# A hybrid decoder layer in fp32: the first activations in eight pieces, and an up projection with stationary weights

## The reference

```python
h = rms_norm(x, ln_mix_w)                      # x: 256 x 2048
proj = h @ w_in                                # 2048 x 9216, the first product
...                                            # pooling branch, HGRN2 branch, gates, w_out
h2 = rms_norm(x, ln_ffn_w)
u = causal_depthwise_conv(h2 @ w_up, conv_w, conv_b)   # 2048 x 11008, 3 taps over tokens
u_gate, u_val = jnp.split(u, 2, axis=-1)
x = x + (jax.nn.silu(u_gate) * u_val) @ w_down         # 5504 x 2048
h3 = rms_norm(x, ln_ple_w)
x = x + jax.nn.sigmoid(h3 @ w_ple_gate) * (p @ w_ple)
return rms_norm(x, ln_final_w)
```

## Time and profile before

| | us |
|---|---|
| median of 3 runs (1482.78 to 1483.22) | 1483.19 |
| the profiled execution, its own time | 1483.09 |
| its span, first to last instruction | 1481.3 |
| PE busy in it | 1460.6 (99%) |
| DVE, ACT, POOL busy | 872.9, 744.3, 126.0 |

### The profile page before, as it was taken

One profiled execution on the slowest core, in us unless ns is written; L12 is line 12 of the kernel. 1 busy time (PEld: TensorE's weight loads), 2 busy tenths in 40 slices (PEclk: granted clock), 3 DMA queues, 4 the chain that ended last, 5 costly groups with the idle time before them and its releaser, 6 DMA issues.

```text
span 1481.3 us, 18755 instructions
## 1 busy us (share of the span) xinstructions
PE 1460.6 (99%) x6814; PEld 1218.5 (82%) x6814; DVE 872.9 (59%) x976; ACT 744.3 (50%) x913; POOL 126.0 (9%) x81
## 2 busy tenths in 40 slices
PE   7999999999999999999999999999999999999997
PEld 5888888888888888888888888888888888888886
DVE  4576676545454545556676666766767555454655
ACT  5555555444444444445555555555555444443544
POOL 1034143100000000000110110100101000000000
PEclk9999999999999999999999999999999999999999
DMA  7755555456666655556656556656555655555653
GB/s 235 248 150 153 159 155 148 144 165 186 197 186 194 189 195 184 190 178 192 184 177 193 184 177 196 181 181 196 175 181 176 202 194 190 196 188 184 223 196 121
DMA packets 189754, 271.88 MB, mean 184 GB/s; under 512 B 11380, under 2 KB 103112, under 8 KB 189568
## 3 DMA queue, kind: packets, MB, share of 16 engines
q1 hardware_dynamic: 189408, 270.88, 58.8%
q0 software_dynamic: 288, 0.21, 0.1%
HBM read 268.95 MB, written 2.10 MB: 183 GB/s over the span
## 4 chain that ended last, share of the span: by engine, by line
PE 97%; DVE 1%; ACT 1%; issue 1%; DMA 0%; POOL 0%; SPq 0%; ACTq 0%; POOLq 0%; DVEq 0%
PE main L528 30%; PE main L529 30%; PE main L530 30%; PE aux L553 3%; PE aux L600 2%; PE aux L634 0%; DMA x_tok<-in_x 0%; PE aux L624 0%; DVE cv L1145 0%; DVE w_lo L1002 0%; ACT w_hi L774 0%; DVE bT L1102 0%; POOL dec L1339 0%; ACT cv L882 0%; PE aux L614 0%
## 5 line engine op out<-in xcount | busy, mean ns | idle before, releaser
L1002 DVE TENSOR_TENSOR w_lo<-raw,w_hi 128x1024 fp32r<-128x1024 f32 x508 | 651.8, 1287 | 550.8 <-ACT w_hi L774 549.5
L774 ACT ACTIVATE w_hi<-raw 128x1024 fp32r<-128x1024 f32 x508 | 535.8, 1055 | 647.6 <-PE main L530 631.5
L528 PE MATMUL main<-w_hi,xT_hi 128*128 128x512 f32 (+1 forms) x1408 | 551.5, 392 | 4.3 <-DVE w_lo L1002 4.3
L530 PE MATMUL main<-w_hi,xT_lo 128*128 128x512 f32 (+1 forms) x1408 | 545.6, 387 | 0.0
L529 PE MATMUL main<-w_lo,xT_hi 128*128 128x512 f32 (+1 forms) x1408 | 545.6, 387 | 0.0
L528 PEld LDWEIGHTS main<-w_hi,xT_hi 128*128 128x128 f32 x1408 | 265.1, 188 | 58.0 <-issue 4.4
L530 PEld LDWEIGHTS main<-w_hi,xT_lo 128*128 128x128 f32 x1408 | 264.9, 188 | 54.4
L529 PEld LDWEIGHTS main<-w_lo,xT_hi 128*128 128x128 f32 x1408 | 265.2, 188 | 51.8
L528 PE MATMUL main<-w_hi,aT_hi 128*128 128x512 f32 x344 | 134.4, 391 | 0.1
L530 PE MATMUL main<-w_hi,aT_lo 128*128 128x512 f32 x344 | 133.9, 389 | 0.0
L529 PE MATMUL main<-w_lo,aT_hi 128*128 128x512 f32 x344 | 133.9, 389 | 0.0
(11 more groups left out here) (166 smaller groups left out, 913.5 us busy)
## 6 DMA issues: line engine op xcount, KB each, us to landing
raw<-in_w_up SPq DMA_DIRECT2D x336, 256.0 KB
raw<-in_w_in SPq DMA_DIRECT2D x144, 512.0 KB
raw<-in_w_down SPq DMA_DIRECT2D x84, 512.0 KB
raw<-in_w_out SPq DMA_DIRECT2D x32, 512.0 KB
raw<-in_w_ple_gate SPq DMA_DIRECT2D x32, 512.0 KB
raw<-in_w_branch_a SPq DMA_DIRECT2D x16, 512.0 KB
raw<-in_w_branch_b SPq DMA_DIRECT2D x16, 512.0 KB
x_tok<-in_x SPq DMA_DIRECT2D x4, 512.0 KB, 8.6
```

Of the source, the lines that this page charges most:

```text
L528: pe.matmul(acc, th, wh, start=first, stop=False)
L530: return pe.matmul(acc, tl, wh, start=False, stop=end)
L774: ac.activation(w_hi[:, u % RING, :, 0:w], raw[:, u % RING, :, 0:w], ACT.Copy).then_inc(hi_full, 1)
L1002: dve.tensor_tensor(w_lo[:, u % RING, :, 0:w], raw[:, u % RING, :, 0:w], w_hi[:, u % RING, :, 0:w].bitcast(F32), ALU.subtract).then_inc(lo ...
```

## The change

**Start.** x comes in eight pieces of 256 columns. SP issues piece 0 first of all, then unit 0 as two loads, then pieces and units in turn; the identity and the norm vector go through ACT's queue. PE does ten matmuls on a constant tile, `junk` (5, 3 and 2, around the first transposes), which nothing reads. The first unit is taken apart (`first_unit`): its first row tile runs product by product as its parts arrive. Piece i+2 is transposed in the middle of unit i.

**Up projection.** `xT_hi` and `xT_lo` become halves of one tile `xT`. In `up_rows` the weights are stationary, 128 columns at a time. `w_hi` meets hi and lo tokens side by side in one matmul of 512 columns, `w_lo` meets the hi tokens in one of 256. A unit is 8 matmuls of 512 and 8 of 256 columns. Results have features on partitions already, four banks for a chunk (all of `main` or all of `aux`, in turn), with the sum still in two halves: ACT copies one half out (`z`), DVE adds the other and multiplies by the row scale, which now varies along the free axis and is held in `rB` (made by two transposes on PE and one copy). The `z_tok` transposes are gone. The half-wide chunk is the first of the 22, not the last.

```diff
-    [(-2, "vec"), (-1, "xT0"), (0, "xT1"), (2, "xT2"), (4, "xT3"), (6, "cvec")]
+    [(-3, "vec"), (-2, "xT0"), (-1, "xT1")] + [(i - 2.5, f"xT{i}") for i in range(2, UK)] + [(6, "cvec")]
...
+    + [(UP + 5, "rB")]
     + [(P_T, "pT")]
...
+
+            def x_piece(i):
+                at = slice(i * FW, (i + 1) * FW)
+                sp.dma_start(x_tok[:, :, at], x_v[:, :, at]).then_inc(x_in[i], 16)
+
+            x_piece(0)
+            at = slice(PROJ[0], PROJ[0] + NCOL)
+            sp.dma_start(raw[:, 0, 0, :], w_in_v[:, 0, at]).then_inc(first_raw, 16)
+            sp.dma_start(raw[:, 0, 1, :], w_in_v[:, 1, at]).then_inc(raw_full[0], 32)
+            for u in range(1, 4):
+                x_piece(u)
                 rows(u, w_in_v, 2 * u, PROJ[0])
-                if u < NQ - 1:
-                    sp.dma_start(x_tok[:, :, cols(u + 1)], x_v[:, :, cols(u + 1)]).then_inc(x_in[u + 1], 16)
+            for i in range(4, UK):
+                x_piece(i)
             for u in range(4, MIX):
...
+            def first_row_tile():
+
+                wh, wl = w_hi[:, 0, 0, :], w_lo[:, 0, 0, :]
+                th, tl = ([t[:, 0, tb * P:(tb + 1) * P] for tb in range(TB)] for t in (xT_hi, xT_lo))
+                pe.wait_ge(xT_hi_ready, 1)
+                pe.wait_ge(first_hi, 1)
+                for tb in range(TB):
+                    pe.matmul(main_acc(0, tb), th[tb], wh, start=True, stop=False)
+                pe.wait_ge(first_lo, 1)
+                for tb in range(TB):
+                    pe.matmul(main_acc(0, tb), th[tb], wl, start=False, stop=False)
+                pe.wait_ge(xT_ready, 1)
+                for tb in range(TB):
+                    pe.matmul(main_acc(0, tb), tl[tb], wh, start=False, stop=False)
+
...
+            def up_rows(j, u, i, it=None, blocks=4):
+
+                pe.wait_ge(lo_full, plus(u + 1, 2 * UK, it))
+                if i == 0 and j:
+                    pe.wait_ge(z_read, plus(j, 2, it))
+                if i == 0 and j == 0:
+                    pe.wait_ge(x_new, 2 * (NQ - 1))
+                for a in range(2):
+                    k = 2 * i + a
+                    for b in range(blocks):
+                        pe.matmul(up_acc(j, b), w_hi[:, u % RING, a, b * P:(b + 1) * P],
+                                  xT[:, k, :, :].rearrange("p h t -> p (h t)"), start=(k == 0), stop=False)
+                    for b in range(blocks):
+                        mm = pe.matmul(up_acc(j, b)[:, 0:SEQ], w_lo[:, u % RING, a, b * P:(b + 1) * P], xT[:, k, 0, :],
+                                       start=False, stop=(k == KD - 1))
+                mm.then_inc(units_done, 1)
+
+            def rstd_rows():
+
+                pe.wait_ge(rstd_ready, 2)
+                for tb in range(TB):
+                    mm = pe.transpose(aux_flat("rB")[:, tb * P:(tb + 1) * P], rstd[:, 1, tb:tb + 1].to_broadcast([P, P]), ident[:])
+                mm.then_inc(aux_ready, 1)
+
...
+            def warm_up(n):
+
+                for _ in range(n):
+                    pe.matmul(main[:, 0, 0, 0:P], junk[:, 0:P], junk[:, 0:P], start=True, stop=True)
+
+            pe.wait_ge(junk_set, 1)
+            warm_up(5)
+            side("vec")
+            warm_up(3)
+            side("xT0")
+            warm_up(2)
+            side("xT1")
             u = 0
+            first_unit()
+            u = 1
             for c in range(C_MIX):
-                for i in range(UK):
...
                 if i == 0:
                     chunk_done(ac, C_UP + j, it)
-                    for tb in range(TB):
-                        ac.activation(z_tok[:, tb, 0:2 * nf * P], main_acc(C_UP + j, tb, 2 * nf * P), ACT.Copy,
-                                      scale=rstd[:, 1, tb:tb + 1]).then_inc(z_ready, 1)
-                if i == 2:
-
-                    name = f"zT{j:02d}"
-                    aux_arrived(ac, name, it)
+                    ac.activation(z[:, 0:2 * nf, :], up_acc(j, slice(0, 2 * nf))[:, :, SEQ:NCOL], ACT.Copy).then_inc(z_half, 1)
+                if i == 1:
+
+                    ac.wait_ge(z_ready, plus(j + 1, 2, it))
...
             def up_post(j, i, it=None):
-                nf = 2 if j < NUP - 1 else 1
+                nf = 2 if j else 1
                 f0 = lambda f: slice(f, f + 1) if it is None else bass.ds(it * 4 + f, 1)
+                if i == 0:
+
+                    dve.wait_ge(z_half, plus(j + 1, 2, it))
+                    zs, acc = z[:, 0:2 * nf, :], up_acc(j, slice(0, 2 * nf))
+                    dve.tensor_tensor(zs, acc[:, :, 0:SEQ], zs, ALU.add).then_inc(z_read, 1)
+                    dve.wait_ge(z_read, plus(j + 2, 2, it))
+                    dve.tensor_tensor(zs, zs, rB[:].rearrange("p (b t) -> p b t", b=1).to_broadcast([P, 2 * nf, SEQ]),
+                                      ALU.mult).then_inc(z_ready, 1)
                 if i == 2:
...
+                if s == UP + 3:
+                    inverse_rms(1)
+                if s == UP + 6:
+                    aux_arrived(dve, "rB")
+                    dve.tensor_copy(rB[:], aux_flat("rB")[:, 0:SEQ]).then_inc(z_read, 1)
...
```

More of the change, by code:

```diff
@@ L151 @@
     + [(out_slot(n) + 1, f"x1T{n}") for n in range(NQ)]
-    + [(up_slot(j) + 1, f"zT{j:02d}") for j in range(NUP)]
+    + [(UP + 5, "rB")]
     + [(P_T, "pT")]
@@ L280, in build @@
         aux_ready = sem("aux_ready")
[L282 removed]
+        x_in = [sem(f"x_in{i}") for i in range(UK)]
+        junk_set, first_raw, first_hi, first_lo = map(sem, ("junk_set", "first_raw", "first_hi", "first_lo"))
         const_in, vec_in, late_in, p_in, lnf_in, out_done = map(
@@ L781, in store, with hi_blocks @@
                     ac.activation(dst(tb), main_acc(c, tb), func, scale=rstd[:, norm, tb:tb + 1]).then_inc(done, 1)
-            def hi_blocks(name, dst, first, vec, done):
+            def hi_blocks(name, dst, first, vec, done, n=4):
                 aux_arrived(ac, name)
-                for b in range(4):
-                    ac.activation(dst[:, first + b, :], aux_blocks(name)[:, b, :], ACT.Copy,
+                src = aux_banks(name) if n == 2 else aux_blocks(name)
+                for b in range(n):
+                    ac.activation(dst[:, first + b, :], src[:, b, :], ACT.Copy,
                                   scale=vecT[:, vec + b:vec + b + 1]).then_inc(done, 1)
@@ L955, in _ @@
                         up_post(j - 1, i, it)
-            for s in range(DOWN - UK, UNITS - SPLIT_TB):
+            for s in range(DOWN, UNITS - SPLIT_TB):
                 slot(s)
```

183 lines of the change are left out of this document (109 added, 74 removed).

## The result

The changed kernel takes 1472.9 us (1471.42 to 1474.0), against 1483.2 before: a ratio of 0.9931, 95% interval [0.9917, 0.9944]. Repeated in a later session it took 1472.54 (1470.88 to 1474.12), 0.9930 [0.9917, 0.9944]. So it is 10.3 us faster. 16.3 were forecast, and the time lies 1.4 us above the range given.

The account below looks back on a forecast made before the run. PE's queue was taken to bound the kernel: 1483.1 - 11.2 (up projection) + 0.5 (waits with the half-wide chunk first) - 5.5 (start) = 1466.9 us, range 1462 to 1471.5.

Parts of the forecast that it names:

- Price of a matmul: Up projection on PE: 226.9 ns per 512-column and 119.8 ns per 256-column matmul, giving 22.19 us per full chunk.
- The paragraph on the operand layout: Up projection: stationary weights might expose weight loads, 188 instead of 120 ns per 256-column matmul; cost taken as 0.
- The observable I named: Up projection: 256-column matmuls at 150 ns or more would show the forecast wrong.
- Transposes gone: Up projection on PE: dropping the z_tok transposes saves 18.7 us.
- old stalls: Old half-wide chunk: PE's waits there disappear, saving 1.1 us.
- rB: Up projection on PE: two transposes for rB and the wait around them add 0.3 us.
- half-wide chunk: Now first in the up projection: 12.3 us of PE work, plus 0.5 us for new waits.
- Rivals 3 to 7: PE stalls 1469.4 (0.07); pieces useless 1472.4 (0.06); DVE bound 1511 (0.03); weight loads show 1561 (0.02); fixed cost vanishes 1431 (0.02).
- The start: Kernel start: first real matmul at about 8.3 us, first chunk ending at 35.3 instead of 40.8, a gain of 5.5 us.
- rival 1: Start gives only 3 us: first unit stays at 427 ns, x1 lands 1 to 1.5 us late; 1469.4 us, chance 0.13.
- rivals 1 and 4: Start: gives little, 1469.4 us, chance 0.13; or eight pieces of x bring nothing, 1472.4 us, chance 0.06.
- the term of 1.2 us: Start: PE's slow-clock stretch in the first unit, taken at half of the earlier 2.3 us.

Follow-up runs that it names:

- all_512: Changed kernel with every w_lo product taken over 512 columns instead of 256, so all matmuls of a unit have one size; 1612.68 us (one execution).
- all_256: Changed kernel with every 512-column matmul of the up projection cut into two of 256 with the same weights; 1485.69 us (one execution).
- no_junk: Changed kernel without the matmuls on the constant tile at the start; 1472.95 us.
- after_again: The changed kernel itself, unaltered, run once more on another chip; 1472.54 us.
- x_pair: Changed kernel with the second piece of x issued directly behind the first, ahead of the first rows of input weights; 1471.63 us.
- eight_a: Changed kernel with all eight 512-column matmuls of a unit first, then the eight of 256, rows as outer loop; 1470.1 us.
- still_x: Changed kernel with pieces of xT as stationary operand of the up projection in place of the weights, its result left out; 1472.26 us (one execution).
- moving_w: Changed kernel with w_hi as moving operand of the up projection in place of xT, its result left out; 1470.62 us (one execution).
- only_hi: Changed kernel without the 256-column matmuls, so the product with w_lo is left out of the up projection; 1419.02 us.

## Why the prediction was wrong, step by step

- **Price of a matmul: the step that failed.** "So a matmul costs its columns and some 13 ns on top" holds for streams of one size without a break, where I had read it (226.7 and 120.0 ns in `all_512` and `all_256`). The changed unit mixes the two, and I multiplied 64 x 0.2269 + 64 x 0.1198 without a bound for that. What the runs showed in its place is 232.4 and 118.5 ns, 33 ns more for a unit. The trace of before had the hint: 314, 232 and 231 ns behind the transposes, and 113 and 119 for the first two 256-column matmuls at 1122.18. I averaged over 45 matmuls that stand clear of both. The chunk is 22.46 and not 22.19: 5.6 us of the miss. The paragraph on the operand layout bounded the wrong thing, the weight load, and took 0, rightly for loads. The observable I named ("256-column matmuls at 150 ns or more") did not catch it; the other, 22.2 us a chunk, did.
- **Transposes gone, old stalls, rB, half-wide chunk**: right. The half-wide chunk took 12.66 us where the terms gave 12.3 + 0.5; the profile has no wait of PE there for rB or weights, and the two pauses of 0.2 us are most of the difference to 12.3. Rivals 3 to 7 did not happen. DVE took 16.3 us of a chunk, less than the 18.1 allowed.
- **The start: right in the middle execution, short in the profiled one.** The first chunk was forecast to end at 35.3; it ended at 35.12 in the middle of eleven executions, within 0.2, and at 36.70 in the one profiled for the changed kernel. That the gain is still 5.1 and 3.6 at the up projection, and not 5.7 and 4.1, is the new wait for `tok`: I looked for waits only up to the first chunk, and put what came behind it at nothing without a row. The landing of piece 1 at 7.3 was at the early end of what came (7.5 in `no_junk`, 9.22 in the changed kernel). I gave one number from one execution's curve, where a spread of 1.7 us belonged to it, and the range had only 1 to 1.5 us for it, in rival 1. Medians give 3.6 to 4.8, by which kernel they are taken against. The times of rivals 1 and 4 (1469.4, 1472.4) come nearer to the result than mine. Rival 1 did happen in part in the profiled execution (piece 1 landed 1.9 us late, the first row tile stayed at 427 ns), but most of the miss is in the loop, which neither of them touches.
- **Clock**: the term of 1.2 us was right in the profiled execution (slow spacing to 12.4) and near 0 in `after_again`. Neither mattered much, since a faster first row tile waits for piece 2. The Trainium skill (TensorE: Matmul & The Clock Gate, section What's actually happening) says that the moment of release varies from run to run; by that, the traces agree: the changed kernel's first four matmuls of that row tile took 1.86 us in one execution (10.08 to 11.94) and 1.01 in the other (8.69 to 9.70).
- **The 2.5 ns of the Trainium skill** (the same page, section Back-to-back issue gap, which gives it for isolated matmuls): one size alone gives 226.7 and 120.0 ns, 13 ns above the columns at 2.4 GHz, also with stationary weights. 2.5 ns is seen in no run here.
- **The range**: 1462 to 1471.5 took in waits and landings, but nothing for a matmul's price in the new mixture. The missing term has one sign in the changed kernel's order and in every other order tried (+13 to +53 ns a unit), and it takes the time out.

## What to carry to other kernels

A price read in a stream of equal instructions is a price for that stream. Look in the trace for what follows a break in it, too. Where a change mixes sizes, leave a term for it: here 33 ns a unit of 2.8 us, 1.2%, and try the orders that the program allows; eight and eight gave 2.8 us here, two and two in one accumulator 3.8. At a start, move first what PE waits for, then look at the next thing that lands: of three edits here none moved the end by more than the executions of one kernel differ among themselves. And before you credit an edit with a microsecond, see where in the trace it lies: in `x_pair` it lay in a loop that the edit hadn't touched.

## What the runs showed of the hardware that I had not expected

- The first five 512-column matmuls behind 256-column ones take 228 to 236 ns instead of 227 (`eight_a`), at a granted clock of 1.00 in the loop. With weights or x held, and x or w_hi streamed, the first four lie at 224 to 236 (`still_x`, `moving_w`). Behind a wait of PE it is much the same (224 to 240 in a unit of `only_hi`). A 256-column one just behind a 512 takes 113 to 119 instead of 120.
- One size alone is exact: 1765 starts of 512 columns in `all_512` (700 to 1100 us) lie 225 to 228 ns apart, 3333 of 256 in `all_256` 119 or 120.
- One and the same loop ran at 2807 ns a unit in four profiled executions and at 2800 in two others, each time to within 1 ns all through the loop.
- The same start, executed eleven times, enters the up projection anywhere in 2.2 us, and the landing of one 256 KB piece of x moves with it: 9.22 us in one execution, before 8.24 in another of the same kernel, 7.46 in `no_junk`.
